# A weight ring of four half blocks, loaded for most weights in whole blocks of 1 MB

## The chip, the core and the metric

The kernel runs on one core of a Trainium2 chip. The metric is the device time in microseconds of one execution. Lower is better. The core has TensorE (PE), VectorE (DVE), ScalarE (ACT), GpSimd (POOL) and SyncE (SP), and 16 DMA engines that move data between the chip's memory and SBUF for all of them.

## The reference, cut to what matters

Two layers over a sequence of 256 tokens of width 1024, in float32. Each layer normalises, multiplies by one wide input projection, runs three mixers on its parts, multiplies by an output projection, and adds the result. It then looks up experts (PEER): queries are another product with a 1024 x 1024 matrix, top-16 of product keys choose 16 experts for each of 8 heads and each token, and each expert is a row of 1024 numbers in each of two tables.

```python
for layer in range(DEPTH):                       # 2
    proj = rms_norm(h, norm1_g[layer]) @ w_in[layer]
    qkv_a, z_a, a_a, b_a, u_s, q_c, k_c, v_c = jnp.split(proj, split_at, axis=-1)
    o_a, o_b, o_c = gdn_mixer(...), s5_mixer(...), diff_attn_mixer(...)
    h = h + jnp.concatenate([o_a, o_b, o_c], axis=-1) @ w_out[layer]
    h = h + peer_ffn(rms_norm(h, norm2_g[layer]), peer_wq[layer], keys, u_tab, v_tab)
# peer_ffn: q = xt @ wq; experts = top 16 of product keys, for each head
#   act = gelu(u_tab[expert] . xt); y = sum over (gate * act) * v_tab[expert]
```

## The kernel before, in words

The work is cut into four iterations, i = 0 to 3: layer i // 2, and half i % 2 of the sequence (128 tokens, one for each partition). An iteration has a mixing part (`mix`, `attention`) and an expert part. The expert part is a stream: GpSimd issues, for every token at once, one gather of 128 rows of the u table and one of the v table in turn (512 KB each, `u_gather`, `v_gather`), 128 of each kind per iteration. The u rows land in a ring of 7 (`uring`), VectorE takes the dot product with each token (line 1306) and so frees the slot (`dot_done`). The v rows land in a ring of 11 (`vring`), and TensorE multiplies them in by fours (`values`), which frees their slots (`v_used`). GpSimd waits for the slot before each gather.

The mixing part of iteration 0 runs alone. Those of iterations 1, 2 and 3 run beneath the gathers of the iteration before. Each engine has its own instruction order, written when the kernel is built: `place` gives each step of the mixing part a position among the 128 steps of the gather stream, and `Stages.advance` puts it there. On TensorE a group of `values` comes after every fourth step, so a few steps of mixing lie between two groups. An engine works strictly in its order, so a step that waits holds up everything behind it.

The weights come through a ring of their own, `wring`, with four slots of 512 KB (`WRING = 4`). All matrices lie in memory in blocks of 256 columns: 128 rows of 8192 bytes, 1 MB. A block is read in two halves, each 128 pieces of 4096 bytes. `CHUNKS` lists the halves in the order of use: 11 blocks of the input projection (u, qkv0 to qkv2, z, v0, v1, q0, q1, k0, k1), one chunk `glu`, the output projection's four blocks (all second halves, then all first halves), and four blocks of the queries (wq0 to wq3). That makes 39 chunks for each iteration. SyncE goes through the list (lines 405 to 414). Before the load of chunk q it waits until q - 3 chunks are done, that is until the chunk four back has left its slot:

```python
if q >= WRING:
    sp.wait_ge(chunk_done.sem, q - WRING + 1)
```

TensorE waits in `chunk_in` (line 444) for the chunk's own slot, and adds one to `chunk_done` after its last matmul. `fill` multiplies a chunk with channels as the output's partitions (eight products), `fill_tokens` with tokens as the output's partitions (four products). In the profile a product in float32 shows as two matmul records, so a chunk is 16 records of 128x128 in `fill` and 8 of 128x256 in `fill_tokens`. All of them carry line 433, where the helper `mm` is.

The input projection's order on TensorE is: u, the small product for a and b, qkv0, qkv1, qkv2 with a product of the S5 mixer (`bu`) between, the first half of z, then a sum of gates (line 541) that needs a copy made by ScalarE, the second half of z, and so on. SyncE loads the norm's gain (line 417) and, after the first chunks, the second half of x (line 419) in between.

Of the kernel before, what the change touches and what calls it, by code (L numbers as in the profile page):

```python
# [11 lines left out]
TB = SEQ // P  # L12
# [11 lines left out]
TOPK = 16  # L24
# [14 lines left out]
IN_COLS = {"u": 1032, "qkv0": 0, "qkv1": 256, "qkv2": 512, "z": 768,  # L39
           "v0": 2312, "v1": 2568, "q0": 1288, "q1": 1544, "k0": 1800, "k1": 2056}  # L40
BLOCKS = list(IN_COLS) + [f"out{i}" for i in range(4)] + [f"wq{i}" for i in range(4)]
NB = len(BLOCKS)


CHUNKS = [(b, half) for b in IN_COLS for half in range(2)] + [("glu", 0)]
CHUNKS += [(f"out{b}", half) for half in (1, 0) for b in range(4)]
CHUNKS += [(f"wq{b}", half) for b in range(4) for half in range(2)]
NC = len(CHUNKS)
AT = {name: n for n, name in enumerate(CHUNKS)}

NI = DEPTH * TB
NP = NI * PH // 2
PAIR = 2 * TOPK
URING, VRING, WRING = 7, 11, 4
END = 1.0e9
LAST_V = PAIR * (NP - 1)
URING_LAG = PAIR - URING

# [38 lines left out]
class Stages:  # L97
# [5 lines left out]
    def advance(self, limit):  # L103

        while self.parts:
            part = min(self.parts, key=lambda one: one[1])
            if part[1] > limit:
                return
            part[1] = next(part[0], END)

# [6 lines left out]
def _build(nc, ctx, x, w_blocks, cols_d, rows_d, keys_d, u_tab, v_tab, cst_d, fin_d, out):  # L117
    def sb(name, shape, dt=F32):
        return ctx.enter_context(nc.sbuf_tensor(name, shape, dt))[(slice(None),) * len(shape)]
# [34 lines left out]
    wring = sb("wring", [P, WRING, 4, BLK])  # L154
# [5 lines left out]
    def row(name):  # L160
        return rows[:, ROWS[name][0]:ROWS[name][1]]
# [104 lines left out]
    w_in = [signal(f"w_in{s}") for s in range(WRING)]  # L266
# [10 lines left out]
    chunk_done = signal("chunk_done", NC)  # L277
# [112 lines left out]
    @block.sync  # L390
    def _(sp):
        def params(layer):
            sp.dma_start(cols[:, :], cols_d[layer, :, 0:HELD_COLS]).then_inc(params_in.sem, 16)
            sp.dma_start(sa[:, 1024:1536], cols_d[layer, :, HELD_COLS:HELD_COLS + 512]).then_inc(params_in.sem, 16)
            sp.dma_start(rows[:, :], rows_d[layer, :, 0:HELD_ROWS]).then_inc(params_in.sem, 16)
            sp.dma_start(keysT[:, :, :].rearrange("p h n -> p (h n)"), keys_d[layer, :, :]).then_inc(params_in.sem, 16)

        sp.dma_start(h[:, 0, :], x[0, 0:P, :]).then_inc(x_in[0].sem, 16)
        sp.dma_start(cst[:, 0:CST["perm"][0]], cst_d[:, 0:CST["perm"][0]]).then_inc(cst_in.sem, 16)
        params(0)  # L400
        for i in range(NI):
            if i == TB:
                sp.wait_ge(*sc_done(0, 2))
                params(1)
            for c, (name, half) in enumerate(CHUNKS):
                q = i * NC + c
                if q >= WRING:
                    sp.wait_ge(chunk_done.sem, q - WRING + 1)
                if name == "glu":
                    src = cols_d[i // TB, :, COLS["glu"][0]:COLS["glu"][1]]  # L410
                else:
                    src = w_blocks[(i // TB) * NB + BLOCKS.index(name), :, 1024 * half:1024 * half + 1024]
                sp.dma_start(wring[:, q % WRING, :, :].rearrange("p k c -> p (k c)"), src
                             ).then_inc(w_in[q % WRING].sem, 16)
                if (name, half) == ("out3", 1):
                    sp.wait_ge(*ao_done(i, 1))
                    sp.dma_start(g2, rows_d[i // TB, :, HELD_ROWS:NROWS]).then_inc(g2_in.sem, 16)
                if q == 2 * WRING:
                    sp.dma_start(h[:, 1, :], x[0, P:2 * P, :]).then_inc(x_in[1].sem, 16)

        sp.wait_ge(hn2_ready.sem, NI)
        sp.dma_start(g2, fin_d).then_inc(fin_in.sem, 16)
        sp.wait_ge(final_ready.sem, 1)
        sp.dma_start(out[0, 0:P, :], hn[:, :]).then_inc(out_done.sem, 16)
        sp.wait_ge(final_ready.sem, 2)
        sp.dma_start(out[0, P:2 * P, :], hnT[:, :, :].rearrange("p k t -> p (k t)")).then_inc(out_done.sem, 16)
        sp.wait_ge(out_done.sem, TB * 16)
# [3 lines left out]
    def _(pe):  # L431
# [11 lines left out]

        def chunk_in(i, name, half):
            q = i * NC + AT[name, half]
            pe.wait_ge(w_in[q % WRING].sem, 16 * (q // WRING + 1))
            return wring[:, q % WRING, :, :]

        def fill(i, name, half, o, fresh):
# [311 lines left out]
        def attention(i):  # L761

            t = i % 2
            rs = rounds(i)
            yield place(i, 66.8)
            pe.wait_ge(*yT_ready(i, 1))
            mm(M2, two0, row("glb"))
            w = chunk_in(i, "glu", 0)
            for k in range(2):
                ins = mm(M2, s5w[:, k, :], w[:, 2 * k:2 * k + 2, :].rearrange("p k c -> p (k c)"), False)  # L770
            ins.then_inc(chunk_done.sem, 1)
            yield place(i, 69)
            pe.wait_ge(*glu_out(i, 1))
            pe.wait_ge(*fill_act(i, 6))
            if t == 1:
                pe.wait_ge(inter_ready.sem, i // 2 + 1)
            scores_of(i, rs[0], *round_heads(i, rs[0]))
            if t == 1:
                yield place(i, 71.3)
                pe.wait_ge(att_exp.sem, rs[0] + 1)  # L780
                scores_of(i, rs[1], *round_heads(i, rs[1]))
                yield place(i, 74.3)
                pe.wait_ge(att_exp.sem, rs[1] + 1)
                turn_probs(i, rs[0], *round_heads(i, rs[0]), M3)
            yield place(i, 76.3)
            turn_probs(i, rs[-1], *round_heads(i, rs[-1]), M2)
            yield place(i, 78.2)
            pe.wait_ge(pT_ready.sem, rs[-1] + 1)
            for hd in range(HEADS):
                for kb_ in range(t + 1):  # L790
                    ins = mm(M3[:, hd * P:(hd + 1) * P], pT[:, hd * (t + 1) + kb_, :],
                             vbuf[:, kb_, hd * P:(hd + 1) * P], kb_ == 0)
            ins.then_inc(ao_done.sem, 1)
# [23 lines left out]
        stages = Stages(mix(0), attention(0))  # L817
        stages.advance(END - 1)
        for n in range(NP + 1):
            if n % 4 == 0 and n < NP:  # L820
                b = n // 4
                stages = Stages(mix(b + 1), attention(b + 1)) if b + 1 < NI else Stages()
                if b > 0:
                    spread(b)
            for j in range(PAIR):
                if n > 0 and j % 4 == 3:
                    values(n - 1, j // 4)
                stages.advance(PAIR * (n % 4) + j)
            if n % 4 == 3:
                stages.advance(END - 1)  # L830


    @block.vector
    def _(dve):
# [189 lines left out]
        def mix(i):  # L1024
# [93 lines left out]
            yield place(i, 99)  # L1118
            dve.wait_ge(*chunk_done(i, AT["out3", 0] + 1))
            V.tensor_tensor(h[:, t, :], h[:, t, :], hp, ALU.add).then_inc(resid.sem, 1)  # L1120
# [211 lines left out]
        def final(t, scaled):  # L1332
# [5 lines left out]
            if t == 0:  # L1338
                dve.wait_ge(fin_in.sem, 16)
                dve.wait_ge(xp_ready.sem, NI)  # L1340
            V.scalar_tensor_tensor(scaled, h[:, t, :], rstd, g2, ALU.mult, ALU.mult).then_inc(final_ready.sem, 1)
# [18 lines left out]
        stages = Stages(mix(0), attention(0))  # L1360
        stages.advance(END - 1)
        for n in range(NP):
            if n % 4 == 0:
                b = n // 4
                stages = Stages(mix(b + 1), attention(b + 1)) if b + 1 < NI else Stages(final_first())
            choose = top(n + 1) if n % 4 != 3 else iter(())
            next(choose, None)
            for j in range(PAIR):
                dot(n, j)
# [4 lines left out]
                if j == 26 and n % 4 != 3:  # L1374
                    gates(n + 1)
                if j == PAIR - 1:
                    gelu(n)
                stages.advance(PAIR * (n % 4) + j)
            if n % 4 == 3:
                stages.advance(END - 1)  # L1380
        weights(NP - 1)
# [5 lines left out]
    def _(act):  # L1387
# [71 lines left out]
        def mix(i):  # L1459
# [51 lines left out]
            yield place(i, 44.2)  # L1511
            act.wait_ge(*chunk_done(i, AT["qkv1", 1] + 1))
            if t == 0:
# [17 lines left out]
            yield place(i, 48.2)  # L1531
            act.wait_ge(*chunk_done(i, AT["z", 1] + 1))
            copy(raw[:, 4:6, 3:3 + P], M1[:, 0:256].rearrange("p (c t) -> p c t", c=2))
# [17 lines left out]
            yield place(i, 53)  # L1551
            act.wait_ge(*chunk_done(i, AT["v1", 1] + 1))
            copy(vbuf[:, t, :], M3).then_inc(fill_act.sem, 1)
# [16 lines left out]
            yield place(i, 58)  # L1570
            act.wait_ge(*chunk_done(i, AT["q1", 1] + 1))
            copy(qT[:, :, :], heads4(M3)).then_inc(fill_act.sem, 1)
# [123 lines left out]
        stages = Stages(mix(0), attention(0))  # L1696
        stages.advance(END - 1)
        for n in range(NP):
# [138 lines left out]
```

## Time and profile before

| what | value |
|---|---|
| median of 3 runs | 1852.67 us (1848.2 to 1854.35) |
| the profiled execution's own time | 1830.78 us |
| its span, first to last instruction | 1829.0 us |
| mean granted TensorE clock | 0.745 of full speed |
| TensorE matmul busy | 1025.4 us (56%) |
| VectorE busy | 1091.3 us (60%) |
| GpSimd busy | 985.0 us (54%) |
| data moved | 628.69 MB, mean 344 GB/s |

Times in the profile are microseconds from the first instruction, unless they are said to be nanoseconds. "DMA share" is the mean busy share of the 16 DMA engines. It can read slightly over 1, because the records of two packets can overlap. A packet is one contiguous piece of a transfer, or the write of 4 bytes with which each DMA engine reports that it is done. The idle time of an engine is put down to what ended it, so "[4.47 <-ACT gd L1391]" is 4.47 us of idling that ended when ScalarE's instruction of line 1391 on `gd` was done.

### The profile page before, as it was taken

The numbers are of one execution on the slowest core, as the hardware profiler recorded it, in microseconds if no ns is written. First come the engines' busy times: TensorE is split into PE (matmuls) and PEld (weight loads), VectorE is DVE, ScalarE is ACT, GpSimd is POOL, SyncE is SP. The second block draws the span as 40 slices with busy tenths as digits, with TensorE's granted clock in tenths as the row PEclk, the third lists the DMA queues.
The fourth block names the chain that finished last, engine by engine and source line by source line (L and its number), as shares of the span: only waits on it lengthen the run. The fifth ranks groups of instructions, "written<-read, shape, count | busy, mean of one in ns | idle before, by whom it ended". The sixth has DMA issues, their size and how long they took to land.

```text
span 1829.0 us, 19147 instructions
## 1 busy us (share of the span) xinstructions
PE 1025.4 (56%) x5988; PEld 613.8 (34%) x5988; DVE 1091.3 (60%) x2833; ACT 302.1 (17%) x839; POOL 985.0 (54%) x1028
## 2 busy tenths in 40 slices
PE   5978577865643328975573326987673323232335
PEld 5857555432420006753350004755350000000001
DVE  6522887766575785767345745866556756656430
ACT  4341422220100003322000003313110000000000
POOL 0000455566656565556556764554666666666664
PEclk9998788887866568988786557998887555555656
DMA  6414899999999999988999998997999999998997
GB/s 225 138 36 134 306 354 411 327 338 349 419 419 420 343 357 385 419 339 320 376 419 379 359 383 331 403 384 276 356 419 419 356 380 377 369 371 341 367 366 276
DMA packets 172613, 628.69 MB, mean 344 GB/s; under 512 B 19168, under 2 KB 19168, under 8 KB 172512
## 3 DMA queue, kind: packets, MB, share of 16 engines
q0 software_dynamic: 147456, 536.94, 75.6%
q1 hardware_dynamic: 25056, 90.53, 13.2%
q8 instruction: 48, 0.79, 0.2%
q14 instruction: 53, 0.43, 0.1%
HBM read 626.34 MB, written 1.05 MB: 343 GB/s over the span
## 4 chain that ended last, share of the span: by engine, by line
PE 24%; issue 20%; DVE 20%; another core or an unknown queue 10%; DMA 9%; POOL 9%; ACT 4%; DVEq 3%; ACTq 0%; POOLq 0%; SPq 0%
PE ps L433 24%; DVE uring L1306 9%; DMA uring<-in_u_tab,small 5%; POOL vring L1717 5%; POOL uring L1717 4%; DMA vring<-in_v_tab,small 2%; DMA wring<-in_w_blocks 1%; PE ps L436 1%; ACT gd L1391 1%; DVE sel L1266 0%; DVE sel L1270 0%; DVE small L1274 0%; DVE small L1221 0%; DMA uring<-in_v_tab,small 0%
## 5 line engine op out<-in xcount | busy, mean ns | idle before, releaser
L1717 POOL DMA_INDIRECT uring<-in_u_tab,small x512 | 493.9, 965 | 556.9 <-DVE small L1306 201.1
L1306 DVE CUSTOM_DVE_ANT_0 uring<-uring,ps 128x1024 f32<-128x1024 f32 x512 | 613.9, 1215 | 233.1 <-DMA uring<-in_u_tab,small 131.3
L433 PE MATMUL ps<-vring,wmat 128*32 128x512 f32 x2008 | 383.3, 861 | 524.5 <-DMA vring<-in_v_tab,small 300.5
L1717 POOL DMA_INDIRECT vring<-in_v_tab,small x502 | 481.5, 959 | 266.8 <-issue 139.7
L433 PEld LDWEIGHTS ps<-vring,wmat 128*32 128x32 f32 x2008 | 75.7, 138 | 775.4 <-issue 749.6
L433 PE MATMUL ps<-hnT,wring 128*128 128x128 f32 x1536 | 211.7, 294 | 53.8 <-issue 42.8
L433 PEld LDWEIGHTS ps<-hnT,wring 128*128 128x128 f32 x1536 | 195.5, 205 | 78.3 <-issue 62.4
L433 PE MATMUL ps<-wring,hnT 128*128 128x256 f32 x448 | 115.1, 406 | 29.0 <-ACT hnT L1391 16.5
L433 PEld LDWEIGHTS ps<-wring,hnT 128*128 128x128 f32 x448 | 87.5, 203 | 56.1 <-ACT hnT L1391 20.2
L433 PE MATMUL ps<-gd 128*128 128x128 f32 x544 | 82.6, 309 | 37.5 <-ACT gd L1391 19.2
L433 PEld LDWEIGHTS ps<-gd 128*128 128x128 f32 x544 | 77.7, 220 | 58.9 <-issue 37.4
L1391 ACT ACTIVATE gd<-ps 128x512 f32<-128x512 f32 (+1 forms) x82 | 47.8, 586 | 203.5 <-remote 84.6
L1707 ACT ACTIVATE small<-small 128x32 f32<-128x32 f32 x16 | 3.7, 230 | 391.9 <-issue 340.2
L433 PE MATMUL ps<-cst 128*128 128x512 f32 x80 | 49.2, 700 | 15.5 <-issue 14.1
L842 DVE TENSOR_TENSOR h<-h,ps 128x1024 f32<-128x1024 f32 x4 | 4.9, 1220 | 79.7 <-PE ps L433 50.5
L436 PE MATMUL ps<-cst,hn 128*128 128x128 f32 x72 | 14.6, 361 | 57.0 <-ACT hn L1391 28.4
L1681 ACT ACTIVATE small<-small 128x16 f32<-128x16 f32 x32 | 6.6, 209 | 240.3 <-issue 202.9
L1306 DVE DVE_READ_ACCUMULATOR2_ANT small<- 128x1 f32 x512 | 42.1, 82 | 0.4 <-issue 0.4
L1217 DVE MAX8 small<-scores 128x8 f32<-128x128 f32 x64 | 14.0, 281 | 44.7 <-issue 17.9
L433 PE MATMUL ps<-sa,cz 128*32 128x128 f32 x256 | 35.5, 296 | 8.4 <-DVEq L991 6.3
L433 PEld LDWEIGHTS ps<-sa,cz 128*32 128x32 f32 x256 | 29.1, 119 | 15.0 <-issue 13.6
L436 PEld LDWEIGHTS ps<-cst,hn 128*128 128x128 f32 x72 | 11.4, 187 | 63.7 <-DVEq L1117 31.3
(281 smaller groups left out, 1129.2 us busy)
## 6 DMA issues: line engine op xcount, KB each, us to landing
wring<-in_w_blocks SPq DMA_DIRECT2D x152, 512.0 KB
uring<-in_u_tab,small POOLq DMA_INDIRECT x512
vring<-in_v_tab,small POOLq DMA_INDIRECT x502
wring<-in_cols SPq DMA_DIRECT2D x4, 512.0 KB
sa<-in_rows SPq DMA_DIRECT2D x4, 512.0 KB
h<-in_x SPq DMA_DIRECT2D x2, 512.0 KB, 4.4
keysT<-in_keys SPq DMA_DIRECT2D x2, 512.0 KB
rows<-in_rows SPq DMA_DIRECT2D x2, 486.0 KB
```

Source lines behind the costliest of these rows:

```text
L433: return nc.tensor.matmul(o, a, b, start=start, stop=True, skip_group_check=True)
L436: return nc.tensor.transpose(o, a, ident)
L842: V.tensor_tensor(h[:, t, :], h[:, t, :], yp, ALU.add).then_inc(y_read.sem, 1)
L1217: V.max(sv[:, hd, a, 0:8], S[:, hd, a, :])
L1306: V.tensor_tensor_reduce(row_, row_, xp, 1.0, 0.0, ALU.mult, ALU.add, dots[:, j:j + 1]).then_inc(dot_done.sem, 1)
L1391: return S.activation(dst, src, ACT.Copy, scale=scale)
L1681: S.activation(gate[:, hd, :], gate[:, hd, :], ACT.Exp, accum_out=gz[:, hd:hd + 1])
L1707: S.activation(gt, gt, ACT.Tanh, scale=GELU).then_inc(gelu_tanh.sem, 1)
L1717: nc.gpsimd.indirect_dma_start(dst, None, table, bass.IndirectOffsetOnAxis(ap=index, axis=0)).then_inc(done.sem, 16)
```

## The change

The 11 blocks of the input projection and the four of the queries are loaded whole, one transfer of 128 rows of 8192 bytes into two neighbouring slots of the ring. A chunk `pad` that loads nothing is put after `glu`, so that there are 40 chunks for each iteration and each pair begins at an even slot. The wait before a pair is for one chunk more than before: both slots must be free. Both halves of a block wait on the semaphore of the pair's first slot, and the table `LANDED` says which value. The last matmul of `glu` counts for two chunks. Matmuls, their order and everything else stay.

```diff
-CHUNKS = [(b, half) for b in IN_COLS for half in range(2)] + [("glu", 0)]
+CHUNKS = [(b, half) for b in IN_COLS for half in range(2)] + [("glu", 0), ("pad", 0)]
 CHUNKS += [(f"out{b}", half) for half in (1, 0) for b in range(4)]
 CHUNKS += [(f"wq{b}", half) for b in range(4) for half in range(2)]
+WHOLE = [name for name, half in CHUNKS if half == 0 and (name in IN_COLS or name[0:2] == "wq")]
+def landings():
+
+    count, out = [0] * WRING, []
+    for q in range(NI * NC):
+        name, half = CHUNKS[q % NC]
+        slot = q % WRING
+        if name == "pad":
+            out.append(None)
+        elif name in WHOLE and half == 1:
+            out.append(out[q - 1])
+        else:
+            count[slot] += 16
+            out.append((slot, count[slot]))
+    return out
+LANDED = landings()
...
                 q = i * NC + c
+                wide = 2 if name in WHOLE else 1
+                if name == "pad" or wide == 2 and half == 1:
+                    continue
                 if q >= WRING:
-                    sp.wait_ge(chunk_done.sem, q - WRING + 1)
+                    sp.wait_ge(chunk_done.sem, q - WRING + wide)
...
-                    src = w_blocks[(i // TB) * NB + BLOCKS.index(name), :, 1024 * half:1024 * half + 1024]
-                sp.dma_start(wring[:, q % WRING, :, :].rearrange("p k c -> p (k c)"), src
-                             ).then_inc(w_in[q % WRING].sem, 16)
+                    src = w_blocks[(i // TB) * NB + BLOCKS.index(name), :, 1024 * half:1024 * (half + wide)]
+                s = q % WRING
+                sp.dma_start(wring[:, s:s + wide, :, :].rearrange("p s k c -> p (s k c)"), src
+                             ).then_inc(w_in[s].sem, 16)
...
         def chunk_in(i, name, half):
             q = i * NC + AT[name, half]
-            pe.wait_ge(w_in[q % WRING].sem, 16 * (q // WRING + 1))
+            slot, value = LANDED[q]
+            pe.wait_ge(w_in[slot].sem, value)
             return wring[:, q % WRING, :, :]
...
-            ins.then_inc(chunk_done.sem, 1)
+            ins.then_inc(chunk_done.sem, 2)
```

The last two lines are in `attention`, after the products with `glu`.

## Rows read from the trace of the kernel before

**Rows 1.** Stretches: engines' busy us (instructions), granted TensorE clock, DMA share, GB/s.

```profile
0.00:186.00 186.00, 143.93 (x926) 124.30 (x926) 77.66 (x285) 68.37 (x189) 0.20 (x4) 0.92 0.39 134
186.00:1372.00 1186.00, 723.61 (x4330) 457.08 (x4334) 777.41 (x2009) 221.27 (x616) 694.20 (x719) 0.78 0.95 369
```

**Rows 2.** The page's DMA queues: packets, MB, share of 16 engines.

```profile
q0 software_dynamic: 147456, 536.94, 75.6%
q1 hardware_dynamic: 25056, 90.53, 13.2%
```

**Rows 3.** Stretches in which weights are loaded beside gathers, columns as in Rows 1.

```profile
225.00:245.00 20.00, 14.41 (x89) 12.05 (x88) 18.47 (x48) 9.47 (x21) 7.27 (x7) 0.85 1.02 417
...
715.00:785.00 70.00, 64.52 (x481) 48.79 (x480) 52.08 (x118) 23.02 (x69) 37.59 (x37) 1.00 1.03 419
1130.00:1155.00 25.00, 24.31 (x171) 19.32 (x171) 18.85 (x56) 14.56 (x38) 10.72 (x11) 0.94 0.97 368
...
1346.00:1371.00 25.00, 20.53 (x151) 17.55 (x154) 11.58 (x40) 2.65 (x5) 14.08 (x15) 0.84 1.03 420
```

**Rows 4.** The chain that ended last, 1125 to 1160: start us, us, what.

```profile
1130.31 24.31 PE ps L433 x171
```

**Rows 5.** Waits: us in total, times, longest us.

```profile
PE ps L433 <- DMA wring<-in_w_blocks: 7.8, 9, 2.1
```

**Rows 6.** DMA queues in 748 to 756: packets, MB, share of 16 engines.

```profile
q1 hardware_dynamic: 275, 1.06, 32.2%
```

**Rows 7.** DMA queues in 1396.6 to 1397.1.

```profile
q14 instruction: 1, 0.01, 3.9%
```

**Rows 8.** Timeline of SyncE, in narrow windows: start us, us of one issue.

```profile
32.55 0.33 SPq L413 DMA_DIRECT2D wring<-in_w_blocks  x1
...
228.54 0.33 SPq L413 DMA_DIRECT2D wring<-in_w_blocks  x1
...
718.94 0.33 SPq L413 DMA_DIRECT2D wring<-in_w_blocks  x1
...
754.43 0.33 SPq L413 DMA_DIRECT2D wring<-in_w_blocks  x1
...
1130.44 0.33 SPq L413 DMA_DIRECT2D wring<-in_w_blocks  x1
...
1142.32 0.33 SPq L413 DMA_DIRECT2D wring<-in_w_blocks  x1
...
1359.83 0.33 SPq L413 DMA_DIRECT2D wring<-in_w_blocks  x1
```

**Rows 9.** DMA queues in 757.6 to 760.5.

```profile
q1 hardware_dynamic: 143, 0.52, 44.2%
```

**Rows 10.** Timeline of TensorE: start us, us, shape, instructions [idle before <-releaser].

```profile
37.22 1.89 PE L433 MATMUL ps<-wring,hnT 128*128 128x256 f32 x8
47.60 0.59 PE L433 MATMUL ps<-small,cst 128*128 128x4 f32 x2 [8.49 <-ACT gd L1391]
...
241.22 0.59 PE L433 MATMUL ps<-small,cst 128*128 128x4 f32 x2 [4.47 <-ACT gd L1391]
...
723.59 1.89 PE L433 MATMUL ps<-wring,hnT 128*128 128x256 f32 x8
...
1136.40 2.05 PE L433 MATMUL ps<-hnT,wring 128*128 128x128 f32 x16
...
1146.97 1.89 PE L433 MATMUL ps<-wring,hnT 128*128 128x256 f32 x8
1148.80 1.92 PE L433 MATMUL ps<-vring,wmat 128*32 128x512 f32 x16
...
1361.73 3.84 PE L433 MATMUL ps<-hnT,wring 128*128 128x128 f32 x32
1367.69 2.90 PE L433 MATMUL ps<-hnT,wring 128*128 128x128 f32 x16 [2.12 <-DMA wring<-in_w_blocks]
```

**Rows 11.** The page's DMA issues: KB each, median us from issue to landing.

```profile
h<-in_x SPq DMA_DIRECT2D x2, 512.0 KB, 4.4
```

More of the change, by code:

```diff
@@ L49 @@
 AT = {name: n for n, name in enumerate(CHUNKS)}
+WHOLE = [name for name, half in CHUNKS if half == 0 and (name in IN_COLS or name[0:2] == "wq")]
+PAIR = 2 * TOPK
 NI = DEPTH * TB
 NP = NI * PH // 2
-PAIR = 2 * TOPK
 URING, VRING, WRING = 7, 11, 4
+def landings():
[12 more added lines that the diff above has]
+LANDED = landings()
 END = 1.0e9
```

## The prediction, made before the changed kernel ran

> **What bounds the kernel now.** I read the stretches first, then the DMA queues, then the chain and the waits. The first 186 us (the first half sequence's projections, attention and queries) run with the DMA engines 0.39 busy; the next 1186 us, in which the expert rows are gathered while the other three iterations' projections run beneath them, have a share of 0.95 [rows 1]. The gathers are 536.94 MB on their queue, everything SyncE loads is 90.53 MB [rows 2]. So most of the time is a stream of gathers that wants the DMA engines, and weights are a guest on it. Where weights are loaded the stream is mostly at its ceiling: 417 and 419 GB/s at a share of 1.02 to 1.03 in three of the four stretches shown, but 368 GB/s at 0.97 in 1130 to 1155 [rows 3]. There the chain that ended last runs through TensorE alone, 24.31 us in one piece of 171 matmuls [rows 4]: the gathers wait until TensorE has used up value rows. All of TensorE's waits on weights are 7.8 us in 9 pieces, 2.1 the longest [rows 5]. Weight waits are thus no bound today; a change of them matters only where TensorE is the chain, and a change of DMA time only where the share is 1.
>
> **What is removed.** 15 blocks in each of 4 iterations go as one transfer of 128 rows of 8192 bytes instead of two of 128 rows of 4096: 60 issues fewer, 60 x 128 rows fewer. A weight row now costs, by 1.06 MB (259 rows) in 32.2% of 16 engines over 8 us, 0.322 x 128 / 259 = 0.159 us, its share of completion packets within [rows 6]. A row of 8192 bytes stands in this trace only as an instruction fetch: one packet of 0.01 MB was 3.9% of 16 engines over 0.5 us, 0.312 us [rows 7]. Two short rows are 0.318, so a pair saves 0.006 us; the rounding of both shares makes that 0 to 0.012. Eight pairs fall to each engine per block: 0.05 us a block, 0 to 0.1. Over 60 blocks that is 3 us of DMA time, 0 to 6, and it counts only where the engines are full; 44 or so of the blocks are loaded there. I take -3 for all, since a weight landed is also out of the stream sooner. SyncE's own issues lie on nothing: it waits most of the time.
>
> **What is added: the first half comes late.** Before, a half block is issued when the chunk four back is done. Now a pair is issued when the chunk three back is done, that is when its second half was issued before, and its first half can't be used before all 1 MB has landed. The second halves never wait again. How long does a load take? Issued at 754.43 [rows 8], one transfer's whole 128 rows (143 packets of its queue) lie in 757.6 to 760.5, at 44.2% of the engines [rows 9]: 6.1 us beside gathers, of which the last 2.6 are its rows alternating with gathered ones. With long rows each alternation is 0.312 + 0.160 instead of two of 0.320: the 1 MB takes 6.1 + 8 x 0.152 = 7.3 us. If long rows were cut in two by the engines it would be 6.1 + 8 x 0.320 = 8.7. I take 7.3, because the fetch went as one packet. The Trainium skill (DMA: Bandwidth & Descriptors, Queues, rings and completion order) says each engine goes round its queues packet by packet, and in SWDGE vs HWDGE vs iDMA that a packet is preferably at most 4096 bytes; by the first alone the long row gets a double turn (7.3), by the second it may not (8.7). No run so far decides it.
>
> Now each burst of back-to-back blocks, by TensorE's starts and SyncE's issues [rows 8, 10]:
> - First iteration, no gathers. A 512 KB load lands 4.4 us after its issue [rows 11], so 1 MB 4.4 + 8 x 0.152 = 5.6. The gate block z is tightest: issued at 32.55, landed at 38.2, wanted at 37.22, 1 us late. Behind it TensorE sits idle 8.49 us on ScalarE until 47.60. Nothing. If that cover were gone: 1 us.
> - Second iteration, z: 228.54 + 7.3 = 235.8, and a further 1.0 because the block two places before it is in the same position (an estimate, from the 1.3 of the fourth iteration below): 236.8. It runs 2 us and the next matmul is at 241.22 after 4.47 us of idling on ScalarE. Nothing; uncovered 2.1.
> - Third iteration, z, with the same 1.0: 718.94 + 1.0 + 7.3 = 727.2 against 723.59: 3.6 late. Queued behind it on TensorE are 16 matmuls of gathered value rows, so rows of the value ring come free 3.6 us later; at 715 to 785 the stream is full [rows 3], and the gathers already issued carry it over. Nothing; uncovered 3.6.
> - Fourth iteration: qkv1 1130.44 + 7.3 = 1137.7 against 1136.40, 1.3 late; z 1142.32 + 1.3 + 7.3 = 1150.9 against 1146.97, 3.9 late in all. The same value matmuls are queued behind it, and here the stream is not full and the chain is TensorE. All 3.9 counts.
> - End of the fourth iteration, queries: wq3 1359.83 + 7.3 = 1367.1 even without earlier delay, against about 1363.65 (half of the piece from 1361.73): 3.5 late; it waited 2.12 for its second half before, so TensorE is 1.4 to 3.4 later than now (the larger with 2.0 from wq2 ahead of it). While it stood still for 2.12 us the stream stayed at 420 GB/s [rows 3], so a wait of this size doesn't show. Nothing; uncovered 3.4. The queries of the second and third iterations are alike, 3.4 each uncovered.
>
> The output blocks still load in halves; the unused fourth slot makes one more of them wait for the GLU chunk, which is long done when the output projection begins. Nothing.
>
> **Sum.** -3 + 3.9 = +1 us on the profiled execution: 1830.78 becomes 1831.8. The median of the runs shown is 1852.67, 1.012 times that, so 1853.7. Bounds of the terms: DMA time -6 to 0, late first halves 0 to 20 (3.9 + 3.6 + 2.1 + 3 x 3.4).
>
> **A rule against it.** The last bullets rest on rows; beside them the Trainium skill (Perfetto Trace Analysis, DMA Optimizations) has both signs: batching from 2 KB to 4 or 8 KB can raise throughput, splitting lets some start sooner if the engines are mostly idle. Here a full stream already moves 419 GB/s with 4 KB rows, which leaves the first little to raise, and the second is the late first half, though the engines are not idle.
>
> **The rivals.** 0.3% (5.5 us) is about what a measurement of this kernel can tell from no change.
> - *Late first halves reach the path* (slower). The rings hold 7 and 11 rows; if their reserve is smaller in the other bursts than the full stream suggests, up to all 20 us count: 1830.78 + 20 - 3 = 1847.8, 1869.9 by the median. It decides from 8.5 of the 20 us on; the half, with 11.5 - 3 = +8.5, gives 1861.3. For it: the fourth iteration is such a place, and DMA share 1.03 is an average over many us. Against: the stream stayed full through a 2.12 us stop. Chance 0.20.
> - *Long rows are cut.* No DMA time is saved and each stall is 1.4 longer; the fourth iteration's two make 3.9 + 2.8 = 6.7: 1837.5 to 1837.8, 1859.8 by the median. Against it stands the fetch in one packet. Chance 0.10.
> - *The stream gains and the stalls hide* (faster). -6 from rows, and the 2.12 us wait on a second half gone: -8, 1822.8, by the median 1844.6. For it: the share of 0.95 over 1186 us, and rings that absorbed 2 us before. Against: it wants the upper end of a rounding. Chance 0.17.
> - *The fixed part of a transfer counts.* 4.4 us to landing [rows 11] less 8 x 0.159 of moving is 3.1 us per removed transfer; all 60 exposed would be 186 us, 1645, by the median 1665. Against: several transfers overlap, or the share could not be 1.03. Chance 0.03. The Trainium skill (DMA: Bandwidth & Descriptors, Anatomy of one DMA) has 2.0 us fixed plus bytes at 436 GB/s: an estimate by that page is 2 us a block, 120 us, on the same condition.
> - *The forecast*, +1 us: 0.50.
>
> **How the numbers follow.** The likeliest case gives 1853.7; its own range, with a scatter of 3 us to each side and its terms' ends, is 1848 to 1859. For 8 in 10 it must reach halfway into the late-halves case and into the cut rows, and to the faster case: 1845 to 1863. By cases: the forecast's 0.50 is 0.42 same and 0.04 each beyond; late halves 0.18 slower, 0.02 same; cut rows 0.05 and 0.05; the gain 0.11 faster, 0.06 same; the fixed part 0.03 faster. Faster 0.18, same 0.55, slower 0.27.
>
> **What the profile of the changed kernel would show.** The queue of SyncE's loads falls from 25056 packets by 60 x 144 = 8640 to 16416 with the same 90.53 MB, and 60 of its packets' groups are 8 KB long; were rows cut, the packets would be 24096. A full stretch with weights has a few GB/s above 419 if long rows are cheaper, 419 if not. TensorE's waits on weights rise from 7.8 to some 20 us, all on first halves, the longest 3 to 4 us at z and wq3; none at a second half. In the fourth iteration's first burst the chain's TensorE piece shows a wait on weights inside it. The forecast is wrong if GB/s in the bursts falls below 400 where it was 419 (the reserve was too small), or if the weight queue's share falls well below 13% (long rows are much cheaper than a fetch).

## The result, and the profile after

| | before | after |
|---|---|---|
| median, same chip | 1844.88 us (1835.34 to 1854.35, 13 runs) | 1861.24 us (1852.77 to 1869.64, 13 runs) |
| the profiled execution | 1830.78 us | 1853.31 us |

The ratio is 1.0093 [1.007, 1.0117]: slower by 0.9%, some 17 us; the profiled executions differ by 22.5 us. All ratios here are taken without the slowest executions (those over 1.5% above the fastest of their kernel), so some differ from the quotient of the medians beside them. The time lies in the forecast's range, but not in its likeliest case, which was no change. The profiled execution of before, at 1830.78 us, is faster than every one of its 13 runs, so the pair of traces shows rather more loss than the runs do.

The page's DMA queues (packets, MB, share of 16 engines) and its DMA issues:

```profile
q0 software_dynamic: 147456, 536.94, 75.1%
q1 hardware_dynamic: 16416, 90.53, 12.8%
...
wring<-in_w_blocks SPq DMA_DIRECT2D x60, 1024.0 KB
wring<-in_w_blocks SPq DMA_DIRECT2D x32, 512.0 KB
```

Against [rows 2], SyncE's queue has the same bytes in 16416 packets, as worked out: the long rows are not cut. Its engine time is 0.128 x 1851.5 = 237.0 us against 0.132 x 1829.0 = 241.4, so 4.4 us less (the rounding of both shares leaves 2.6 to 6.3), for which I had 3 (0 to 6). What the change removes came as computed. The stretches, with columns as in the rows before the prediction:

```profile
186.00:1372.00 1186.00, 716.00 (x4181) 450.62 (x4180) 765.14 (x1968) 219.50 (x613) 679.55 (x703) 0.79 0.94 361
...
225.00:245.00 20.00, 13.78 (x100) 12.29 (x100) 18.47 (x49) 10.27 (x24) 7.28 (x7) 1.00 1.01 410
715.00:785.00 70.00, 63.88 (x440) 48.88 (x440) 47.61 (x111) 28.52 (x88) 33.96 (x35) 0.96 0.99 384
1150.00:1175.00 25.00, 20.37 (x137) 14.87 (x136) 13.59 (x39) 8.75 (x19) 9.25 (x9) 0.93 1.00 386
1365.00:1400.00 35.00, 24.35 (x176) 20.70 (x176) 18.09 (x58) 2.88 (x5) 18.79 (x20) 0.85 1.02 420
```

The stream of gathers has 361 GB/s where it had 369 [rows 1], and GpSimd has issued 703 instructions against 719. In the third iteration's burst of weights (715 to 785) it falls to 384 GB/s, where it was 419 [rows 3]; at the queries (1365 to 1400) it is 420, as it was.

Where the time is lost shows in how many instructions GpSimd has issued by a given time (the number in brackets ahead of the clock). Before:

```profile
186.00:700.00 514.00, 281.87 (x1611) 167.21 (x1612) 361.07 (x991) 86.39 (x236) 307.20 (x319) 0.74 0.96 370
186.00:880.00 694.00, 418.29 (x2526) 264.56 (x2526) 487.75 (x1296) 140.56 (x401) 407.46 (x421) 0.78 0.95 369
186.00:1130.00 944.00, 529.71 (x3131) 321.53 (x3131) 619.45 (x1630) 158.09 (x440) 560.38 (x580) 0.75 0.95 370
186.00:1400.00 1214.00, 734.83 (x4402) 460.04 (x4402) 801.52 (x2064) 224.15 (x623) 713.61 (x738) 0.78 0.95 371
186.00:1600.00 1414.00, 797.47 (x4686) 472.73 (x4690) 922.13 (x2357) 229.86 (x639) 847.37 (x879) 0.75 0.96 371
```

After:

```profile
186.00:700.00 514.00, 283.74 (x1614) 169.34 (x1612) 361.74 (x995) 85.58 (x233) 305.44 (x316) 0.77 0.95 367
186.00:880.00 694.00, 420.94 (x2506) 268.98 (x2504) 475.47 (x1275) 141.08 (x402) 396.09 (x407) 0.80 0.93 359
186.00:1130.00 944.00, 532.75 (x3108) 323.50 (x3107) 613.89 (x1617) 158.60 (x441) 551.28 (x570) 0.76 0.94 364
186.00:1400.00 1214.00, 737.22 (x4338) 468.89 (x4340) 780.02 (x2020) 221.80 (x617) 694.58 (x719) 0.79 0.94 363
186.00:1600.00 1414.00, 804.64 (x4650) 482.71 (x4648) 910.65 (x2333) 230.16 (x639) 828.78 (x861) 0.76 0.94 365
```

By 700 us it is 3 gathers behind, by 880 it is 14, by 1130 10, by 1400 19, by 1600 18. A gather of 524 KB at 419 GB/s is 1.25 us, so 18 of them are 22.5 us: the whole difference of the profiled executions. It arises in the mixing of the third iteration (700 to 880) and of the fourth (1130 to 1400). One trace against one can mislead here, since the runs of one kernel spread over some 18 us. But the two later traces of the changed kernel (below) agree on the place: from 700 to 880 us GpSimd issues 102 instructions in the kernel before, and 91, 89 and 90 in the three traces of the changed one.

TensorE's waits on weights, over the whole execution, and what waits on TensorE and VectorE in turn (us in total, times, longest):

```profile
POOL uring L1742 <- DVE small L1331: 210.2, 73, 14.8
...
DVE small L1022 <- PE ps L457: 39.3, 5, 13.4
PE ps L457 <- DMA wring<-in_w_blocks: 31.9, 15, 4.7
```

Weight waits went from 7.8 us [rows 5] to 31.9. The first two kinds were 201.1 us (longest 11.4) and 29.6 us (4 times, longest 10.3) before. Whether they are the route is asked below. Some places of the weight waits, on TensorE's timeline:

```profile
240.30 1.99 PE L457 MATMUL ps<-wring,hnT 128*128 128x256 f32 x8 [2.12 <-DMA wring<-in_w_blocks]
242.13 0.28 PE L457 MATMUL ps<-small,cst 128*128 128x4 f32 x2
...
735.04 3.49 PE L457 MATMUL ps<-wring,hnT 128*128 128x256 f32 x8 [2.86 <-DMA wring<-in_w_blocks]
738.47 1.92 PE L457 MATMUL ps<-vring,wmat 128*32 128x512 f32 x16
...
1158.69 3.84 PE L457 MATMUL ps<-hnT,wring 128*128 128x128 f32 x32 [1.80 <-DMA wring<-in_w_blocks]
1165.26 3.42 PE L457 MATMUL ps<-wring,hnT 128*128 128x256 f32 x8 [2.73 <-DMA wring<-in_w_blocks]
...
1393.43 5.47 PE L457 MATMUL ps<-hnT,wring 128*128 128x128 f32 x32 [4.67 <-DMA wring<-in_w_blocks]
```

Each of these waits is ahead of a block's first half: the second half follows in the same group (the x32 rows are both halves of one block). The second iteration's sum of gates (242.13) had 4.47 us of idling ahead of it [rows 10] and has none now; it starts 0.9 us later than it did.

**Two routes to the gathers.** I had looked for it in the bursts of weights only. In this pair of traces a second part of the loss comes some 90 us later, at the attention step, where the stream runs dry in both kernels. Stretches of before:

```profile
810.00:825.00 15.00, 13.28 (x75) 8.15 (x75) 8.52 (x27) 7.07 (x25) 4.18 (x5) 0.92 0.51 188
1236.00:1248.00 12.00, 12.00 (x53) 5.77 (x52) 7.66 (x23) 3.70 (x12) 3.63 (x4) 1.00 0.42 146
```

and of after:

```profile
820.00:840.00 20.00, 16.25 (x89) 11.12 (x89) 8.87 (x28) 7.77 (x26) 4.53 (x5) 0.83 0.48 175
1258.00:1272.00 14.00, 14.00 (x60) 7.56 (x59) 7.03 (x18) 4.63 (x13) 3.00 (x4) 0.92 0.37 131
```

In time of a full stream (419 GB/s) the first pair lost 15 x (1 - 188/419) = 8.3 us and loses 11.6 now, the second 7.8 and 9.6. Who waits for whom there, before in 800 to 822:

```profile
POOL uring L1717 <- DVE small L1306: 11.4, 1, 11.4
DVE small L997 <- PE ps L433: 10.3, 1, 10.3
```

and after in 812 to 836:

```profile
POOL uring L1742 <- DVE small L1331: 14.8, 1, 14.8
DVE small L1022 <- PE ps L457: 13.4, 1, 13.4
```

VectorE works in order. It stands at line 1022, the maximum over the attention scores, until TensorE has them. Queued behind it are the dot products, which alone free the u ring's 7 slots. GpSimd, and with it the stream, stands 1.1 to 1.4 us longer than VectorE does. In this pair the wait grew by 3.1 us (10.3 to 13.4), GpSimd's by 3.4. The same pair in the fourth iteration went from 9.5 and 10.9 to 12.6 and 14.0.

The two later traces of the changed kernel (`after_again` and `after_third`, below) don't bear this out as the main route. VectorE's wait for the scores was 5.6 and 6.4 us there in the third iteration, less than before, and 12.6 and 8.1 us in the fourth. What grows in every trace with late halves is GpSimd's wait at the v ring for TensorE, the route that the prediction had named. From 700 to 880 us, in the kernel before, the changed one, its two later traces, and a kernel with late halves on short rows (`e1c_short_rows`, below):

```profile
POOL vring L1717 <- PE ps L433: 6.8, 2, 4.1
...
POOL vring L1742 <- PE ps L457: 13.3, 3, 6.4
...
POOL vring L1742 <- PE ps L457: 21.0, 3, 9.9
...
POOL vring L1742 <- PE ps L457: 21.2, 4, 9.2
...
POOL vring L1743 <- PE ps L455: 25.6, 4, 9.6
```

With its waits on dot products (37.1 us before; 46.6, 32.8, 42.2 and 39.5) GpSimd stood 10 to 21 us longer in this stretch, and the 11 to 16 gathers that it was behind are 14 to 20 us of full stream. So the loss in the third iteration is GpSimd standing longer at the two rings; how it is shared between them differs from trace to trace, and of the kernel before there is one trace only.

### The profile page after: what moved, and what is told of

Read it like the earlier page. It is cut to its first block, busy times and chain, and to the rows that moved or that the text cites. A ratio compares the mean times of both kernels' runs of the same rounds, so it can differ in the third digit from the quotient of the medians.

```text
span 1851.5 us, 19087 instructions
## 1 busy us (share of the span) xinstructions
PE 1041.8 (56%) x5988; PEld 625.5 (34%) x5988; DVE 1092.0 (59%) x2833; ACT 302.3 (16%) x839; POOL 984.6 (53%) x1028
## 3 DMA queue, kind: packets, MB, share of 16 engines
q1 hardware_dynamic: 16416, 90.53, 12.8%
## 4 chain that ended last, share of the span: by engine, by line
PE 22%; another core or an unknown queue 20%; DVE 18%; issue 17%; DMA 9%; POOL 8%; ACT 3%; DVEq 3%; ACTq 0%; SPq 0%; POOLq 0%
PE ps L457 21%; DVE uring L1331 8%; POOL vring L1742 5%; DMA uring<-in_u_tab,small 4%; POOL uring L1742 3%; DMA wring<-in_w_blocks 3%; DMA vring<-in_v_tab,small 1%; ACT gd L1416 1%; PE ps L460 1%; DVE small L1257 0%; DVE small L1246 0%; DVE small L1268 0%; ACT sa L1476 0%; DVE sel L1291 0%
## 5 line engine op out<-in xcount | busy, mean ns | idle before, releaser
L457 PE MATMUL ps<-vring,wmat 128*32 128x512 f32 x2008 | 391.6, 858 | 512.5 <-DMA vring<-in_v_tab,small 377.1
L457 PE MATMUL ps<-hnT,wring 128*128 128x128 f32 x1536 | 216.9, 299 | 69.9 <-issue 40.8
L457 PEld LDWEIGHTS ps<-hnT,wring 128*128 128x128 f32 x1536 | 201.4, 211 | 92.3 <-issue 55.1
L457 PE MATMUL ps<-wring,hnT 128*128 128x256 f32 x448 | 119.6, 419 | 37.9 <-ACT hnT L1416 16.1
L1331 DVE DVE_READ_ACCUMULATOR2_ANT small<- 128x1 f32 x512 | 42.2, 82 | 0.7 <-issue 0.6
```

The source lines that it names most:

```text
L457: return nc.tensor.matmul(o, a, b, start=start, stop=True, skip_group_check=True)
L1331: V.tensor_tensor_reduce(row_, row_, xp, 1.0, 0.0, ALU.mult, ALU.add, dots[:, j:j + 1]).then_inc(dot_done.sem, 1)
```

## The experiments

Theory A: the loss is the late first halves, through TensorE's order. Theory B: it is the long rows, which hold the DMA engines from gathered rows for 0.31 us at a time. A third question was which blocks carry the loss. The runs came in four groups, each on one chip and with runs of the kernel before in between. In two groups the kernel before took 1670 us, in two 1861 and 1864; one chip gave both. In what follows a group is named by that time, because it turned out to decide what can be seen in it.

**Pairs with short rows.** The block goes in two transfers of 4096-byte rows again, issued one behind the other once both slots are free, and the first half waits for the second too:

```diff
-        elif name in WHOLE and half == 1:
-            out.append(out[q - 1])
...
-                if name == "pad" or wide == 2 and half == 1:
+                if name == "pad":
...
-                    sp.wait_ge(chunk_done.sem, q - WRING + wide)
+                    sp.wait_ge(chunk_done.sem, q - WRING + (1 if half else wide))
...
-                    src = w_blocks[(i // TB) * NB + BLOCKS.index(name), :, 1024 * half:1024 * (half + wide)]
+                    src = w_blocks[(i // TB) * NB + BLOCKS.index(name), :, 1024 * half:1024 * (half + 1)]
...
             pe.wait_ge(w_in[slot].sem, value)
+            if name in WHOLE and half == 0:
+                slot, value = LANDED[q + 1]
+                pe.wait_ge(w_in[slot].sem, value)
```

> The changed kernel, but a block is again two transfers with rows of 4096 bytes; both are issued together when both slots are free, and the first half still may not be used before both have landed. Only the length of the rows differs from the changed kernel. Theory A (a first half that comes late stops TensorE, and the gathers behind it run dry): 1 MB takes 8.7 us instead of 7.3 beside gathers, so about 13 tight first halves come 1.4 us later still, TensorE's waits on weights go from 31.9 to some 50 us, and the ratio to the kernel before rises from 1.009 to 1.010 to 1.018. Theory B (the long rows themselves hold up the gathers, whose rows of 4096 bytes take turns with them): the loss is gone, 0.997 to 1.003.

**The same, but each half used when it has landed** (the diff without its last three lines).

> As the first kernel here (rows of 4096 bytes, two transfers issued together when both slots are free), but TensorE may use the first half as soon as it has landed. Left of the change is only the later issue of first halves. Theory A: the first half lands 6.1 us after the issue and the second 8.7 us, and it is wanted 1.9 us after the first, so a block costs what a landing after 6.8 us would, instead of 7.3: a little less than the changed kernel, 1.005 to 1.009. Theory B: 0.997 to 1.003. Theory C (the loss is in waiting for the whole block, not in the later issue): 0.998 to 1.003, and the first kernel here keeps it.

**Whole blocks only where TensorE comes late to them**, the others in halves as before:

```diff
-WHOLE = [name for name, half in CHUNKS if half == 0 and (name in IN_COLS or name[0:2] == "wq")]
+WHOLE = ["u", "qkv0", "v0", "v1", "q0", "q1", "k0", "wq0", "wq1"]
```

> The changed kernel with whole loads only where the trace of before had 2 us or more to spare (u, qkv0, v0, v1, q0, q1, k0, wq0, wq1); qkv1, qkv2, z, k1, wq2, wq3 load in halves again. 36 of the 60 long transfers stay. Theory A: nearly all of the loss is gone, 0.998 to 1.003, TensorE's waits on weights are near the 7.8 us of before. Theory B: 36 of 60 long transfers keep 36 of 60 parts of 0.93%, 1.0056.

**Whole blocks only where they are tight:**

```diff
-WHOLE = [name for name, half in CHUNKS if half == 0 and (name in IN_COLS or name[0:2] == "wq")]
+WHOLE = ["qkv1", "qkv2", "z", "k1", "wq2", "wq3"]
```

> The other part alone: whole loads only for qkv1, qkv2, z, k1, wq2, wq3, 24 of the 60. Theory A: these carry the loss, 1.006 to 1.010, with waits on weights of 25 us or more. Theory B: 24 of 60 parts, 1.0037.

All four ran in one group, with the kernel before at 1670.62 us (33 runs):

| kernel | median us | ratio [95%] | TensorE's waits on weights |
|---|---|---|---|
| pairs, short rows | 1670.97 | 1.0004 [0.9994, 1.0013] | 42.4 us, 21 times, longest 5.0 |
| own halves | 1672.31 | 1.0015 [1.0006, 1.0024] | 15.7, 14, 1.8 |
| roomy blocks whole | 1670.31 | 1.0003 [0.9994, 1.0012] | 4.4, 6, 1.7 |
| tight blocks whole | 1670.09 | 1.0003 [0.9994, 1.0012] | 23.6, 13, 3.2 |

By the letter of what was expected, the first two ratios are what B had and a miss for A, the third is what A had, and the last is a miss for both. The weight waits come where A put them, though fewer than the 50 us it had: 42.4 us with late halves on short rows, few where only roomy blocks are whole. But they cost nothing here. The kernel with pairs of short rows, its waits and a stretch:

```profile
POOL uring L1743 <- DVE small L1332: 159.8, 114, 5.4
...
PE ps L455 <- DMA wring<-in_w_blocks: 42.4, 21, 5.0
...
DVE uring L1332 <- issue: 9.1, 55, 0.5
```
```profile
760.95 1.29 DVE L1023 TENSOR_REDUCE small<-ps 128x4 f32<-128x512 f32 x2 [4.08 <-PE ps L455]
```
```profile
186.00:1372.00 1186.00, 737.18 (x4534) 449.70 (x4534) 862.75 (x2197) 225.38 (x628) 778.72 (x806) 0.80 1.02 409
```

The engines are full (1.02) throughout, the burst of 715 to 785 runs at 419 GB/s, VectorE's waits for scores beneath the gathers are 4.1 and 4.0 us instead of 10.3 and 9.5, and GpSimd's longest for dot products is 5.4 instead of 11.4 (up to 9.1 in the other kernels of this level): here the stream does have a reserve that carries it over. These four say that late halves with waits of up to 5 us are free at 1670 us; they can't tell A from B, since there is no loss to be explained. Own halves is 0.15% slower though it waits less than the pairs (15.7 us against 42.4); I have no cause for it.

**The changed kernel again**, as it is, to see its loss on another chip; **and both kernels with a v ring of 8 rows**:

```diff
-URING, VRING, WRING = 7, 11, 4
+URING, VRING, WRING = 7, 8, 4
```

The second pair asks whether the v ring is what passes a late TensorE on to the gathers, as the prediction had it.

> The changed kernel once more, on the chip that this set draws. In the first set the kernel before took 1670.6 us and kept its stream at 419 GB/s almost throughout, where in the measurement of the result it took 1844.9 us with many stretches below 400 GB/s. Theory A (late first halves cost where the stream of gathers has no reserve): on a chip where the kernel before takes about 1670 us the ratio is 0.999 to 1.003; where it takes about 1845 us it is 1.007 to 1.012. Theory B (long rows hold up the gathers wherever they run): 1.007 to 1.012 on either.

> The kernel before with 8 slots instead of 11 in the ring of v rows, so that TensorE's delays reach the gathers sooner. A yardstick for the next kernel: some per cent slower than with 11, 1.005 to 1.04.

> The changed kernel with 8 slots instead of 11 in the ring of v rows. Theory A: with 3 slots less of reserve (3 x 2.5 us of stream) the late first halves, about 32 us of waits, show on any chip: its ratio to the kernel before with 8 slots is 1.004 to 1.010, also where the unchanged pair differs by nothing. Theory B: the same ratio to its yardstick as the changed kernel has to the kernel before.

The kernel before took 1864.38 us here (23 runs). The changed kernel: 1881.29 us, 1.0102 [1.006, 1.0143], weight waits 27.2 us in 17 pieces. The loss repeats, as both theories had it. With 8 v rows the kernel before took 1855.5 (0.9943 [0.9903, 0.9983]), the changed one 1851.32 (0.992 [0.9886, 0.9955]). Both are faster than with 11, where some per cent slower was expected of the first. Between them the change costs nothing that can be seen: 1851.32/1855.5 = 0.998, uncertain by some 0.005 either way. That is a miss for A, by which the loss should have stayed with a smaller ring, and as much for B, by which the ratio should have been that of the changed kernel, 1.0102. Waits of the kernel before with 8 v rows:

```profile
POOL vring L1717 <- PE ps L433: 176.8, 44, 12.8
...
POOL uring L1717 <- DVE small L1306: 59.9, 39, 8.3
```
```profile
827.36 1.29 DVE L997 TENSOR_REDUCE small<-ps 128x4 f32<-128x512 f32 x2 [5.31 <-PE ps L433]
```

GpSimd now stands at the v ring and much less at dot products, and VectorE's waits for scores beneath the gathers are 5.3 and 5.2 us, not 10.3 and 9.5. The long wait at the scores is gone, which would go with the loss being gone; but it was as short in a trace of the changed kernel that did lose (5.6 us in the third iteration), so it doesn't explain it. Nor does the v ring: GpSimd's waits there are 176.8 us here and 174.1 with the change, though weight waits went from 6.9 us to 25.4 (the profiled execution of the latter took 1872.88 us, longer than all its others). Why late halves cost nothing beside 8 v rows is open.

**Pairs with short rows, roomy and tight blocks, a second time.** Meant for a group at 1860 us; the same chip as in the last group now gave 1670.44 for the kernel before (29 runs).

> The kernel with rows of 4096 bytes, both halves issued together and the first used only when both have landed, again, in the hope of a chip like those on which the changed kernel was 1.009 and 1.010. In the first set it fell on a chip where the kernel before takes 1671 us, TensorE has no unexplained gaps and none of four kernels differed by more than 0.2%. If the kernel before takes about 1850 us or more here: theory A (lateness) 1.009 to 1.018; theory B (long rows) 0.996 to 1.004. If it takes about 1670 us: 1.000 by both.

> Whole loads only for the nine blocks with time to spare, again. Where the kernel before takes 1850 us: theory A 0.997 to 1.004 with TensorE's waits on weights below 15 us; theory B 1.0056 (36 of 60 long transfers).

> Whole loads only for the six blocks that TensorE wants soon, again. Where the kernel before takes 1850 us: theory A 1.006 to 1.011; theory B 1.0037 (24 of 60). In the profile the attention step of VectorE (it reads the scores) should wait 2 to 4 us longer on TensorE than in the kernel before, and GpSimd's longest wait on VectorE should grow by as much: that is the way by which TensorE's lateness reaches the gathers if the ring of v rows has no part in it, as the kernels with 8 slots suggest.

Measured: 1670.42 us, 1.0001 [0.9992, 1.001] (waits on weights 43.9 us); 1668.95, 0.9992 [0.9983, 1.0001] (5.7 us); 1669.36, 0.9994 [0.9984, 1.0004] (22.4 us). The first group again, and no more. The growth of the wait for scores that was expected of tight blocks whole isn't seen at this level: 4.4 and 4.2 us in the first group, as with roomy blocks (4.4 and 4.2). These pages also give the time to landing of both kinds of load. From the page of the kernel with roomy blocks whole, in this group:

```profile
wring<-in_w_blocks SPq DMA_DIRECT2D x80, 512.0 KB, 7.1
wring<-in_w_blocks SPq DMA_DIRECT2D x36, 1024.0 KB, 8.0
```

Beside a full stream half a block lands in 7.1 us and a whole one in 8.0, as the median (7.3 and 8.3 in the first group).

**Pairs with short rows, a third time, with the changed kernel beside it:**

> Beside the changed kernel on one chip: late first halves with rows of 4096 bytes. Theory A: at least the ratio of the changed kernel, since a first half is usable 1.4 us later still. Theory B (long rows): 0.996 to 1.004 while the changed kernel has 1.009. Where the kernel before takes about 1670 us: 1.000 by both.

> The changed kernel. Where the kernel before takes about 1850 us: 1.007 to 1.012. Where it takes about 1670 us, a chip on which the changed kernel itself has not been timed yet: 0.998 to 1.002 by theory A, since there the stream stays full while TensorE waits some 30 us on weights; theory B leaves 1.007 to 1.012 there too.

Now the kernel before took 1861.19 us (15 runs). Pairs with short rows: 1885.69 us, 1.0131 [1.0105, 1.0158]. The changed kernel: 1874.37, 1.004 [1.0002, 1.0079], less than in the other two groups (1.0093, 1.0102) and less than the 1.007 to 1.012 expected. The short rows lose too, and more. So long rows aren't needed for the loss. B had them at the time of the kernel before and falls; A had them slower, as they are. Their waits, the stretch, and TensorE at the third iteration's z:

```profile
POOL uring L1743 <- DVE small L1332: 205.5, 76, 14.8
...
PE ps L455 <- issue: 170.3, 83, 18.4
...
DVE uring L1332 <- issue: 49.8, 99, 2.9
...
PE ps L455 <- DMA wring<-in_w_blocks: 39.4, 22, 3.5
DVE small L1023 <- PE ps L455: 30.0, 4, 14.0
```
```profile
186.00:1372.00 1186.00, 713.82 (x4122) 448.71 (x4121) 755.72 (x1943) 217.35 (x609) 664.95 (x693) 0.78 0.93 355
```
```profile
739.61 3.45 PE L455 MATMUL ps<-wring,hnT 128*128 128x256 f32 x8 [3.40 <-DMA wring<-in_w_blocks]
```

It is the picture of the changed kernel's first trace: z late by 3.40 us (there 2.86), VectorE at the scores for 14.0 us (13.4), GpSimd behind it for 14.8 (14.8). The changed kernel's trace of this group has z late by 4.17 us and the scores at only 6.4. In the burst of 715 to 785 all of them are below the 419 GB/s of before: 384, 368 and 375 in the three traces of the changed kernel, 365 here. And it is the same program that ran at 1670 us with 42.4 us of weight waits and a share of 1.02. So the weight waits are not the difference between the two levels; a loss goes with them at one and not at the other.

The difference of these two from each other, 1.0131 against 1.004, is more than the 4.4 us of DMA time that long rows save. The pairs with short rows also wait longer on weights (39.4 us in 22 pieces against 33.6 in 17). Whether that explains 0.9% is open.

## Why the prediction came out as it did

**That the time lies in the range is luck in part.** The range, 1845 to 1863, was laid around a median of 1852.67 us for the kernel before; beside the changed kernel it took 1844.88. The measured ratio on the forecast's own base is 1.0093 x 1852.67 = 1869.9 us, outside the range. It is the price of the rival in which all late halves count.

**The step that failed** is the third iteration: "at 715 to 785 the stream is full [rows 3], and the gathers already issued carry it over. Nothing; uncovered 3.6." The size was near (z was 2.86 us late, computed 3.6). The cover was not there: 419 GB/s fell to 384, that is 70 x (1 - 384/419) = 5.8 us of full stream in the burst alone (368 and 375 GB/s in the later traces). This was the prediction's own sign of being wrong, a burst below 400 GB/s. At the attention step 11.6 us were lost instead of 8.3. The mean share of a stretch, 1.03, says that the engines were busy in it. It does not say how many us of issued gathers were in hand at the moment of the stop, and it says nothing of the place 90 us on where nothing is in hand.

**The route was named rightly but not in full.** I followed the late z to the value matmuls queued behind it and to the v ring, and held that the gathers in hand would cover it. GpSimd's waits at the v ring from 700 to 880 us were 13.3 to 25.6 us with late halves, 6.8 before. The other thing that waits for TensorE is VectorE at the scores, and all dot products wait behind VectorE. The chain of waits of before had it, at 800 to 822, as one 10.3 us wait under one 11.4 us wait; it was not read. Where the stream already stands, there should be no cover for further lateness, and in the first pair of traces both waits grew by what TensorE was late; in the other two they didn't grow in the third iteration, so a price for this route is not shown.

**The fourth iteration** was rightly named as a place where lateness counts, with 3.9 us. TensorE stood 1.80 and 2.73 us there, 4.5 in all. From 1130 to 1400 GpSimd fell back by 9 gathers, some 11 us of full stream; since the same clock time is by then an earlier place in the program, a part of that is mere shift. TensorE's lateness itself was near the forecast; by which route it cost more is open. As predicted, the chain that ended last goes through a load of weights there, 9.38 us up to z's start at 1165.26.

**The size of the waits**: forecast some 20 us, measured 31.9 (27.2 and 33.6 in the other two groups). I had 6.1 us for half a block to land and 7.3 for a whole one; beside a full stream they take 7.1 and 8.0. The step between them, 1.2 forecast and 0.9 measured, was right; the base was one transfer read in a window and was 1 us short. 1 us more for each of 15 waits is about the difference. The Trainium skill's 2.0 us fixed plus bytes at 436 GB/s (DMA: Bandwidth & Descriptors, Anatomy of one DMA), from which the prediction's last rival has an estimate, is given there for transfers that GpSimd issues; these are SyncE's.

**What was right.** First iteration: nothing (the sum of gates starts at 47.82 instead of 47.60). Second iteration: the idle time on ScalarE took up all but 0.9 us; 6.2 us of waiting (2.31, 1.79, 2.12) had come in by then, three times what I had, and the cover of 4.47 was used to the end. Queries: 4.67 us of waiting at 1393.43, the stream at 420 GB/s, nothing lost; by 1400 and 1600 us the deficit in gathers is the same, 19 and 18. Second halves of whole blocks never waited. Rows of 8192 bytes are not cut and cost what the one instruction fetch had shown: in 770 to 781 (queues: packets, MB, share)

```profile
q1 hardware_dynamic: 144, 1.05, 22.7%
```

128 rows and their completions took 0.227 x 16 x 11 / 128 = 0.312 us each, the forecast's number to the digit. So the Trainium skill's preference for packets of at most 4096 bytes (DMA: Bandwidth & Descriptors, SWDGE vs HWDGE vs iDMA) is not a limit at which this queue cuts: this trace has 60 x 128 longer ones.

**Which rival it was.** Late first halves reach the path, with chance 0.20. Its price with all 20 us counted and 3 saved was +17, which is what the ratio gives (0.0093 x 1844.88 = 17.2); the profiled executions differ by 22.5. The sum is not proof that all waits count: those of the first and second iterations and of the queries seem not to, so those of the third and fourth must count for more than their own length, in a way that is not shown. The chance of it was too low because the evidence for a reserve was one stop of 2.12 us at the queries, where no attention follows.

**What stays open.** The changed kernel itself did not run in a group at 1670 us. Its two parts did, roomy and tight blocks, at 0.999 to 1.0003, and pairs with short rows at 1.0001 and 1.0004, so no loss is to be expected there, but that is argued. That z and its neighbours carry the loss at 1860 us is read from the trace; the kernels that would separate them met only 1670 us. So did the kernel that uses each half when it has landed. It would tell waiting for a whole block from issuing two halves at once, which might crowd the gathers by itself; this rival stands. A weight ring of six slots, which would give whole blocks the lead that halves had, was not tried. No kernel beat the one before by more than its interval except the two with 8 v rows, for a reason that is not known.

## What to carry to other kernels

A transfer twice as large in a ring of the same bytes starts one consumer step later and is usable one landing later: work out both for each block that is used back to back. The Trainium skill's advice to batch transfers (DMA: Bandwidth & Descriptors, Bandwidth) bought little here: 512 KB ones already made 419 GB/s beside the gathers, and there were 4.4 us of DMA time to win against some 24 us of new waits. A DMA share of 1.03 over a stretch says that the engines were busy, not that a reserve is in hand. To price lateness of an engine, look at every ring whose slots wait for it and at the places where the critical stream already stands waiting for it, however far on; and before one such place is named, take a second trace of the same kernel, for here the wait at the scores was 13.4, 5.6 and 6.4 us in three.

## What the runs showed that I had not expected

**Two levels of one program.** Pairs with short rows took 1670 us in two groups and 1886 in one, on chips whose kernel before took the same 1670 and 1861. The first 186 us, without gathers, are alike. Of the kernel before there is no trace at the lower level; what follows is from the others. Beneath the gathers TensorE has idle time at 1860 us that ends in nothing the profile shows ("issue": 170.3 us in 83 pieces, up to 18.4; 274.1 us in 111 pieces in the kernel before), and at 1670 us no such row among its waits. VectorE's likewise: 49.8 us before its dot products against 9.1. One chip gave both, in different groups. Its cause is open. It matters for what a change is worth: in pairs with short rows 39.4 us of weight waits went with 24.5 us more than the kernel before at the one level, and 42.4 us with 0.4 us more at the other.

**Fewer v rows are not slower.** 8 rows instead of 11 made the kernel before 0.6% faster (0.9943 [0.9903, 0.9983]) in a group at 1864 us.
